# Head pairs in a second attention, and expert values accumulated with features in the partitions

## The reference

```python
s_w = jnp.einsum('bnqhgd,bnkhd->bnhgqk', qb, k_w).astype(jnp.float32) * scale
s_c = jnp.einsum('bnqhgd,bkhd->bnhgqk', qb, k_c).astype(jnp.float32) * scale
s_w = jnp.where(valid[None, :, None, None], s_w, NEG_INF)
p = jax.nn.softmax(jnp.concatenate([s_w, s_c, sink_b], axis=-1), axis=-1)
o = jnp.einsum('bnhgqk,bnkhd->bnqhgd', p_w, v_w) + jnp.einsum('bnhgqk,bkhd->bnqhgd', p_c, v_c)
```

```python
h = jnp.einsum('thkd,td->thk', u_tab[expert], zb).astype(jnp.float32)
act = (gate * jax.nn.gelu(h, approximate=False)).astype(zb.dtype)
return jnp.einsum('thk,thkd->td', act, v_tab[expert])
```

## Time and profile before

| | us |
|---|---|
| median of 3 runs | 4268.56 |
| lowest, highest | 4261.12, 4279.62 |
| the profiled execution | 4257.62 |
| its span, first to last instruction | 4255.8 |
| TensorE busy | 3832.7 (90%) |
| VectorE busy | 2633.9 (62%) |
| ScalarE busy | 1667.1 (39%) |
| GpSimd busy | 624.1 (15%) |
| mean granted clock of TensorE | 0.978 |

### The profile page before, as it was taken

How to read it: one execution, slowest core, us unless ns; L and a number is a source line. 1 busy time by engine, 2 the same in 40 slices (tenths; PEclk the granted TensorE clock), 3 DMA queues, 4 the chain that set the end, 5 groups by cost and what they waited for, 6 DMA issues and landing times. The chain is left out here.

```text
span 4255.8 us, 50533 instructions
## 1 busy us (share of the span) xinstructions
PE 3832.7 (90%) x17626; PEld 2701.9 (63%) x17626; DVE 2633.9 (62%) x5211; ACT 1667.1 (39%) x3644; POOL 624.1 (15%) x665
## 2 busy tenths in 40 slices
PE   6999988999999999998999888788789998887877
PEld 4788765788788865897878744233278787442322
DVE  6877556677565546656347666777553466677774
ACT  3222535323332245543225444444332254444443
POOL 1100000000000000000000143444300002444442
PEclk9999998999999999999999999999999999999999
DMA  5554111355333310553033599999920346999997
GB/s 213 202 184 173 70 40 55 119 181 171 128 141 131 125 61 1 199 186 120 11 129 129 220 420 420 420 420 420 375 80 21 129 146 248 420 420 420 420 420 310
DMA packets 135007, 904.29 MB, mean 212 GB/s; under 512 B 14855, under 2 KB 15879, under 8 KB 35168
## 3 DMA queue, kind: packets, MB, share of 16 engines
q0 software_dynamic: 95552, 620.97, 36.2%
q1 hardware_dynamic: 39200, 280.08, 18.5%
HBM read 899.90 MB, written 5.28 MB: 213 GB/s over the span
## 5 line engine op out<-in xcount | busy, mean ns | idle before, releaser
L2511 PE MATMUL ps<-arena 128*128 128x512 f32 x1640 | 809.8, 622 | 183.1 <-ACT arena L2574 181.5
L2670 DVE CUSTOM_DVE_ANT_0 arena<-arena 128x1024 f32<-128x1024 f32 x410 | 502.5, 1226 | 326.6 <-DMA arena<-peer_uv,arena 325.5
L620 DVE TENSOR_TENSOR w_lo<-wt,w_hi 128x1024 fp32r<-128x1024 f32 x388 | 475.4, 1225 | 351.7 <-ACT w_hi L602 328.1
L2511 PEld LDWEIGHTS ps<-arena 128*128 128x128 f32 x1640 | 292.4, 193 | 628.4 <-ACT arena L2574 402.0
L655 PE MATMUL ps<-h_hi,w_hi 128*128 128x512 f32 (+1 forms) x1744 | 649.4, 372 | 32.5 <-DVE h_lo L742 22.5
L2642 POOL DMA_INDIRECT arena<-peer_uv,arena x410 | 433.4, 1057 | 1583.3 <-DVEq L2633 989.2
L602 ACT ACTIVATE w_hi<-wt 128x1024 fp32r<-128x1024 f32 x388 | 407.6, 1058 | 636.1 <-PE ps L655 607.0
L655 PE MATMUL ps<-h_lo,w_hi 128*128 128x512 f32 (+1 forms) x1744 | 639.5, 367 | 0.0
L655 PE MATMUL ps<-h_hi,w_lo 128*128 128x512 f32 (+1 forms) x1744 | 639.2, 367 | 0.0
L450 PE MATMUL ps<-hT,wt 128*128 128x256 f32 x1632 | 407.0, 387 | 6.1 <-ACT hT L1389 5.1
L655 PEld LDWEIGHTS ps<-h_hi,w_hi 128*128 128x128 f32 x1744 | 332.1, 190 | 94.0 <-issue 17.7
(11 more groups left out here) (342 smaller groups left out, 5453.8 us busy)
## 6 DMA issues: line engine op xcount, KB each, us to landing
wt<-wstream SPq DMA_DIRECT2D x262, 1024.0 KB, 4.9
ada_t<-adastream POOLq DMA_DIRECT2D x133, 512.0 KB, 3.7
arena<-peer_uv,arena POOLq DMA_INDIRECT x410, 20.3
arena<-adastream POOLq DMA_DIRECT2D x11, 512.0 KB, 26.6
bias_by_query<-bias_by_distance POOLq DMA_DIRECT2D x1, 4096.0 KB, 17.3
arena<-bias_by_query POOLq DMA_DIRECT2D x1, 3072.0 KB, 12.1
xT<-tokens SPq DMA_DIRECT2D x1, 2048.0 KB, 15.2
cst<-consts SPq DMA_DIRECT2D x1, 1816.0 KB, 9.0
```

The lines of the kernel that those rows point to most:

```text
L620: self.step(self.dve.tensor_tensor(lo, raw_group(g), hi.bitcast(F32), ALU.subtract))
L2511: ins = pe.matmul(bank, diag[n % DIAGS], row[:, at:at + 512], start=s == 0, stop=s == SLOTS - 1)
L2670: dve.tensor_tensor_reduce(u, u, ztok[:, t], 1.0, 0.0, ALU.mult, ALU.add, hbuf[:, t, s:s + 1]).then_inc(dot_ready.sem, 1)
```

## The change

It makes two edits. In the second joint attention a unit becomes a pair of heads (16 pairs): both heads' scores go to two neighbouring banks, two pairs of banks rotate, the maximum is taken of both at once, the two turn banks serve one pair and are copied out in one instruction, and the values of the two heads go to the two halves of the partitions of one bank. The sink is negated once, and its exponent is formed on VectorE. In the expert layer the roles of the two operands are swapped: the row's 128x128 pieces are the weights and `diag` moves, eight matmuls of 128 columns in place of two of 512, so that the result has features in the partitions, and VectorE adds the banks to `xT` directly. The copy, the transposes and their two signals are gone.

```diff
         oB = MB(8, LAT)
-        N = Carve(U.at)
+        N = Carve()
         b_gain = small[:, 8:9]
-        b_banks = [ps[:, i] for i in range(4)]
-        b_probs = [N(TOK) for _ in range(3)]
-        sinkv = N(8, 4)
-        B_UNITS = [(h, q) for h in range(B_HEADS) for q in range(QT)]
+        b_probs = [N(2, TOK) for _ in range(3)]
+        b_mixed = [N(2, TOK) for _ in range(3)]
+        b_turned = [N(2, 4, P) for _ in range(3)]
+        sinkv = N(8, 4, 2)
+        sink_neg = N(B_HEADS)
+        assert N.at <= SPLIT_END
+        B_PAIRS = [(u, q) for u in range(B_HEADS // 2) for q in range(QT)]
...
         def pe_b_attend(pe, W, mm):
-            n = len(B_UNITS)
+            n = len(B_PAIRS)
             for i in range(n + LAG + 1):
                 if i < n:
-                    h, q = B_UNITS[i]
-                    r = slice((h % 2) * HD, (h % 2 + 1) * HD)
-                    bank, far = b_banks[i % 4], slice((1 - q) * P, (2 - q) * P)
-                    if i >= 4:
-                        pe.wait_ge(SB.raised, i - 3)
-                    mm(bank, qB[r, h // 2, q * P:(q + 1) * P], kD[r, h // 4, :], True, False)
-                    mm(bank[:, far], ident, const("window", q, TOK)[:, far], False, True, SB.scored)
+                    u, q = B_PAIRS[i]
+                    s, far = a_banks[i % 2], slice((1 - q) * P, (2 - q) * P)
+                    if i >= 2:
+                        pe.wait_ge(SB.raised, i - 1)
+                    for x in range(2):
+                        r = slice(x * HD, (x + 1) * HD)
+                        mm(s[:, x, :], qB[r, u, q * P:(q + 1) * P], kD[r, u // 2, :], True, False)
+                    for x in range(2):
+                        mm(s[:, x, far], ident, const("window", q, TOK)[:, far], False, True, SB.scored if x else None)
                 if LAG <= i < n + LAG:
                     u = i - LAG
-                    a, t = a_mixed[u % 3], turn_banks[u % 2]
                     pe.wait_ge(SB.even, u + 1)
-                    for j in range(4):
-                        ins = pe.transpose(t[:, j * P:(j + 1) * P], a[:, j * P:(j + 1) * P], ident)
+                    if u:
+                        pe.wait_ge(SB.kept, u)
+                    for x in range(2):
+                        for j in range(4):
+                            ins = pe.transpose(turn_banks[x][:, j * P:(j + 1) * P],
+                                               b_mixed[u % 3][:, x, j * P:(j + 1) * P], ident)
                     ins.then_inc(SB.turned, 1)
                 if i > LAG:
                     u = i - LAG - 1
-                    h, q = B_UNITS[u]
-                    g = h // 4
-                    r = slice((h % 2) * HD, (h % 2 + 1) * HD)
-                    t, o = turned[u % 4], value_banks[u % 2]
+                    g = B_PAIRS[u][0] // 2
+                    t, o = b_turned[u % 3], value_banks[u % 2]
                     pe.wait_ge(SB.kept, u + 1)
                     if u >= 2:
                         pe.wait_ge(SB.stored, u - 1)
                     for j in range(4):
-                        mm(o[r, 0:P], vB[:, j, g * HD:(g + 1) * HD], t[:, j, :], j == 0, j == 3,
-                           SB.valued if j == 3 else None)
+                        for x in range(2):
+                            mm(o[x * HD:(x + 1) * HD, 0:P], vB[:, j, g * HD:(g + 1) * HD], t[:, x, j, :], j == 0, j == 3,
+                               SB.valued if j == 3 and x else None)
...
         def act_b_attend(act):
-            n = len(B_UNITS)
+            n = len(B_PAIRS)
             for i in range(n + LAG):
                 if i >= LAG:
                     u = i - LAG
                     act.wait_ge(SB.turned, u + 1)
-                    act.activation(turned[u % 4], turn_banks[u % 2].rearrange("p (a b) -> p a b", b=P),
+                    act.activation(b_turned[u % 3], ps[:, 4:6].rearrange("p x (a b) -> p x a b", b=P),
                                    ACT.Copy).then_inc(SB.kept, 1)
                 if i < n:
-                    h, q = B_UNITS[i]
-                    sv = sinkv[:, i % 8, :]
+                    sv = sinkv[:, i % 8]
                     act.wait_ge(SB.peaked, i + 1)
-                    act.activation(b_probs[i % 3], b_banks[i % 4], ACT.Exp, bias=sv[:, 0:1], accum_out=sv[:, 1:2])
-                    act.activation(sv[:, 2:3], v("b_sink", h), ACT.Exp, bias=sv[:, 0:1]).then_inc(SB.raised, 1)
+                    for x in range(2):
+                        act.activation(b_probs[i % 3][:, x, :], a_banks[i % 2][:, x, :], ACT.Exp, bias=sv[:, 0, x:x + 1],
+                                       accum_out=sv[:, 1, x:x + 1])
+                    act.activation(sv[:, 2, :], sv[:, 2, :], ACT.Exp).then_inc(SB.raised, 1)
 
         def dve_b_attend(dve, step):
-            n = len(B_UNITS)
+            step(dve.tensor_scalar(sink_neg, v("b_sink", 0, B_HEADS), -1.0, None, ALU.mult))
+            n = len(B_PAIRS)
             for i in range(n + LAG + 2):
                 if i < n:
-                    h, q = B_UNITS[i]
-                    sv = sinkv[:, i % 8, :]
+                    u, q = B_PAIRS[i]
+                    sv, sink = sinkv[:, i % 8], sink_neg[:, 2 * u:2 * u + 2]
                     dve.wait_ge(SB.scored, i + 1)
-                    top = step.mark(dve.tensor_reduce(sv[:, 0:1], b_banks[i % 4], AX, ALU.max))
+                    top = step.mark(dve.tensor_reduce(sv[:, 0, :], a_banks[i % 2], AX, ALU.max, negate=True))
                 if i >= LAG + 2:
                     x = i - LAG - 2
-                    hx, qx = B_UNITS[x]
-                    r = slice((hx % 2) * HD, (hx % 2 + 1) * HD)
+                    ux, qx = B_PAIRS[x]
                     dve.wait_ge(SB.valued, x + 1)
-                    dve.tensor_copy(oB[r, hx // 2, qx * P:(qx + 1) * P], value_banks[x % 2][r, 0:P]).then_inc(SB.stored, 1)
+                    dve.tensor_copy(oB[:, ux, qx * P:(qx + 1) * P], value_banks[x % 2][:, 0:P]).then_inc(SB.stored, 1)
                 if i < n:
                     step.reached(top)
-                    dve.tensor_scalar(sv[:, 0:1], sv[:, 0:1], v("b_sink", h), -1.0, ALU.max, ALU.mult).then_inc(SB.peaked, 1)
+                    step.reached(step.mark(dve.tensor_tensor(sv[:, 0, :], sv[:, 0, :], sink, ALU.min)))
+                    dve.tensor_tensor(sv[:, 2, :], sv[:, 0, :], sink, ALU.subtract).then_inc(SB.peaked, 1)
                 if 1 <= i < n + 1:
-                    u = i - 1
-                    su = sinkv[:, u % 8, :]
-                    dve.wait_ge(SB.raised, u + 1)
-                    step.reached(step.mark(dve.tensor_tensor(su[:, 3:4], su[:, 1:2], su[:, 2:3], ALU.add)))
-                    step.reached(step.mark(dve.reciprocal(su[:, 3:4], su[:, 3:4])))
-                    dve.tensor_scalar(a_mixed[u % 3], b_probs[u % 3], su[:, 3:4], None, ALU.mult).then_inc(SB.even, 1)
+                    w = i - 1
+                    su = sinkv[:, w % 8]
+                    dve.wait_ge(SB.raised, w + 1)
+                    step.reached(step.mark(dve.tensor_tensor(su[:, 3, :], su[:, 1, :], su[:, 2, :], ALU.add)))
+                    step.reached(step.mark(dve.reciprocal(su[:, 3, :], su[:, 3, :])))
+                    for x in range(2):
+                        ins = dve.tensor_scalar(b_mixed[w % 3][:, x, :], b_probs[w % 3][:, x, :], su[:, 3, x:x + 1], None,
+                                                ALU.mult)
+                    ins.then_inc(SB.even, 1)
...
-        def pe_peer_out(pe, t):
-            pe.wait_ge(y_stored.sem, y_stored.due(pe, 2))
-            for half, bank in enumerate(out_banks(t)):
-                for k in range(4):
-                    m = 4 * half + k
-                    ins = pe.transpose(bank[:, k * P:(k + 1) * P], ztok[:, t, m * P:(m + 1) * P], ident)
-                ins.then_inc(y_turned.sem, 1)
...
-                if (t, h) == (1, 1):
-                    pe_peer_out(pe, 0)
...
                     pe.wait_ge(diag_ready.sem, diag_ready.due(pe))
-                    for bank, at in zip(y_banks(t), (D, D + 512)):
-                        ins = pe.matmul(bank, diag[n % DIAGS], row[:, at:at + 512], start=s == 0, stop=s == SLOTS - 1)
+                    for m in range(DC):
+                        ins = pe.matmul(y_banks(t)[m // 4][:, (m % 4) * P:(m % 4 + 1) * P], row[:, D + m * P:D + (m + 1) * P],
+                                        diag[n % DIAGS], start=s == 0 and m % 4 == 0, stop=s == SLOTS - 1,
+                                        skip_group_check=True)
                     ins.then_inc(row_free, 1)
                     n += 1
                 if scoring:
                     pe_peer_subs(pe, W, mm, l, h + AHEAD, 1)
-            pe_peer_out(pe, 1)
             pe_peer_sums(pe, mm, 1)
...
-                if h == PEER_H - 1:
-                    act.wait_ge(row_free, n)
-                    for half, bank in enumerate(y_banks(t)):
-                        act.activation(ztok[:, t, half * 512:(half + 1) * 512], bank,
```

(14 more changed lines are left out.)

## The result

The changed kernel takes 4237.53 us (median of 5 runs, 4227.70 to 4238.62) against 4268.56 beside it (4261.12 to 4279.62): a ratio of 0.9921, interval 0.9901 to 0.9941, so 25 to 42 us less (by the two medians 31.0). Forecast were 4232 and 4216 to 4252. The profiled execution took 4227.7 us, 29.9 less than that of before; 36.6 were forecast.

What follows compares the result with a forecast made beforehand. TensorE alone bounds the second attention, DMA the expert gathers. Attention 32.9 us off plus stage ends 3.7 makes 36.6, taking the profiled execution from 4257.6 to 4221.0 and the median from 4268.6 to 4232; range 4216 to 4252.

Steps and rivals of the forecast that it cites:

- Period: Second attention: a pair takes TensorE 3.56 us (scores 1.06, windows 0.43, transposes 1.05, values 1.02), where two units took 5.85.
- Fill: Start of the second attention: with only two score banks, pair 2 starts at 5.1 us and pair 5 at 13.9.
- Other engines: Second attention: VectorE about 3.1 us a pair at most and ScalarE about 2.7, both below TensorE's 3.56.
- The slots: Expert gathers: slots stay below DMA's 2.49 us, 2.21 with a query; nothing charged, bounds 0 to 31 us.
- The ends: End of both layers' gather stages: VectorE adds right after the last matmul, 1.83 us off each, 3.7 together.
- The clock at the end: Sums behind layer 1's gathers, earlier at mean clock 0.59: whether it falls there now is unknown, 1.6 us either way.
- rival 1: Expert gathers: TensorE becomes the bound, a pass takes 0.21 us instead of 0.11; 555 us more, 4787; chance 0.07.
- rival 2: Second attention: the two heads' values don't run side by side; period 4.42 us, stretch 74.3, time 4245; chance 0.12.
- Rival 3: Expert gathers: TensorE falls behind in query slots by more than buffers hold; 8 to 40 us given back; chance 0.11.

Runs made afterwards that it cites:

- experiment 3: Changed kernel with each head's window matmul directly after its own score, so a pair's scores are no longer neighbours; 4264.27 us, ratio 0.9992, attention stretch 89.22 us.
- experiment 4: Changed kernel with a pair's value matmuls ordered first head, then second head, instead of alternating; 4243.64 us, ratio 0.9928 to the kernel before, attention stretch 69.60 us.
- experiment 5: Changed kernel with window mask and identity copied to float32r, so each window matmul is one pass instead of two; 4234.17 us, ratio 0.9926, attention stretch 60.53 us.
- experiment 7: Changed kernel with one, or three, extra unread 128x128 matmuls per expert slot; 4235.00 us (ratio 0.9911) with one, 4309.98 us (ratio 1.0078) with three.

## Why the prediction was right

It was right in the total and in what carries it, the attention by pairs; the interval of 25 to 42 us holds the 36.6 forecast. The terms, in the order of the sum:

- **Period, 3.56 forecast, 3.60 measured.** Scores 1.06 and values 1.02 as summed, windows 0.44 for 0.43, transposes 1.07 for 1.05. The prices were rows of the same form elsewhere in this kernel, and experiments 3 and 4 show that the two large ones rest on the order of the instructions, experiment 5 that a pass less is a pass gained.
- **Fill, 13.9 us forecast to pair 5, 15.0 measured.** The chain was as drawn; pairs 2 and 5 of after's weight loads:
```profile
1605.19 0.30 PEld L450 LDWEIGHTS ps<-arena 64*128 64x128 f32 x4 [1.91 <-ACT arena L1324]
1606.89 0.93 PEld L450 LDWEIGHTS ps<-cst 128*128 128x128 f32 x4 [1.40 <-issue]
...
1614.99 0.30 PEld L450 LDWEIGHTS ps<-arena 64*128 64x128 f32 x4 [0.17 <-issue]
```
Pair 2 comes at 5.19 after the start (forecast 5.1). Then scores take 1.70 where others take 1.06 and four window loads 0.93 where others take 0.52: the clock stood at the lower level just there, and the pairs behind it were late. The two traces of experiment 7 have the same attention with the same waits and no such fall; the same loads and the whole stretch in the first of them:
```profile
1608.12 0.30 PEld L450 LDWEIGHTS ps<-arena 64*128 64x128 f32 x4 [1.91 <-ACT arena L1324]
1609.18 0.52 PEld L450 LDWEIGHTS ps<-cst 128*128 128x128 f32 x4 [0.76 <-issue]
...
1616.77 0.30 PEld L450 LDWEIGHTS ps<-arena 64*128 64x128 f32 x4 [0.17 <-issue]
```
```profile
1602.93:1664.83 61.90, 58.43 (x512) 40.11 (x512) 45.23 (x129) 39.57 (x96) 0.00 (x0) 1.00 0.01 2
```
There the scores of pair 2 take 1.06, pair 5 comes at 13.84 after the start, and the stretch is 61.9 at clock 1.00. So the fill was sized rightly, the 1.1 us are the clock, and a wait of TensorE in the fill does not bring the fall about each time. At equal clock the gain is 32.4 where 32.9 was forecast; the rest is the period. In after's trace the stretch is 63.05 and the gain 31.3, but the fall ahead of the attention was shorter there: the part of the stage ahead of it took 22.95 us at a mean clock of 0.85, against 24.31 at 0.79 before. Both together are 32.6 us shorter.
- **Other engines.** VectorE and ScalarE were forecast near 80% in the steady part. Eight rounds of it:
```profile
1620.40:1649.18 28.78, 28.78 (x258) 20.01 (x257) 22.14 (x64) 19.62 (x48) 0.00 (x0) 1.00 0.01 1
```
That is 77% and 68%, or 2.77 us a pair for VectorE, where I had 3.1 with waits on its own results, and 2.45 for ScalarE, where I had 2.7. Neither sets the period.
- **The slots, 0 charged.** A query slot of 2.21 was forecast and 2.22 measured. A pass takes 0.11, about a quarter of the 0.43 of 512 columns, with rows as weights that DMA has just written; a load adds next to nothing. The Trainium skill's rule in TensorE: Matmul & The Clock Gate, Part 3: Packing small matmuls, that loads overlap only where the row group differs, is not borne out for these full-height float32 loads either.
- **The ends, 2 x 1.83 forecast.** Measured 1.75 (3.85 to 2.10) in layer 0 and 1.77 in layer 1. The last slot's 16 passes of 128 columns run 0.06 longer than four of 512, which I had left out. The gather stages are 2.4 and 3.8 us shorter as a whole, 1.5 of the latter from the clock in the norm's sums (next point).
- **The clock at the end, 1.6 us either way.** It went the good way: 16 loads 1.86 us instead of the 3.36 of the earlier trace rows. In 4214 to 4218 the clock is 1.00. That is luck as far as the forecast goes. With the old expert part these loads took 3.36, 3.41 and 1.86 in three traces; with the new one 1.86 in all eight, and whether the change keeps the clock up there was not tested.

The rivals: rival 1 (0.21 per pass) is refuted by the 0.11, and rival 2 by 16 loads in 0.85; experiment 4 shows what a worse order looks like, 0.49 us a pair where the rival had 0.86. Rival 3 is refuted by 1.01 and 419 in the full windows and by gather stages that became shorter, and experiment 7 says how near it was, 0.27 us per query slot. By the two profiled executions the stages that the change touches are 37.4 us shorter (31.3, 2.4 and 3.8), where 36.6 were forecast; 1.5 of the 37.4 are the clock of the last point. At equal clock the attention and the two ends come to 32.4 and 3.5, 35.9 in all. 7.5 us came back in stages that no edit touches, which leaves 29.9. That last part changes sign when the other two executions are paired: 4275.8 against 4232.2 is 43.6 us. One price on record does not come out of its own working: for rival 3, a quarter to all of 0.06 x 512 = 31 us and as much again are, taken literally, 15 to 61 us and not 8 to 40; the forecast's sum does not use it.

## What to carry to other kernels

Take the price of a new instruction pattern from a row of the same shape and the same order elsewhere in the trace, and place matmuls that can share the array directly behind each other: one loop line was worth some 20 of 32 us at equal clock. Where DMA bounds a stage, work added to another engine is free up to a margin that can be measured by adding dummy work until the rate falls; state that margin per slot in the stage's worst part, not as a mean. Before explaining a few microseconds, in stages that no edit touches or in one that an edit does, compare the granted clock of the stretch in both traces, and profile the old kernel a second time.

## What the runs showed that was not expected

- TensorE runs passes of another output half ahead by some four passes: 16 passes in head order take 1.34 us, where the alternating order takes 0.85.
- A change of the array's shape costs 0.17 to 0.19 us at clock 1.00 where it was read, around the values and in experiment 3; at clock 0.50 the same idle time before the value loads is 0.33.
- The changed kernel has 62,653 instructions and fetches 3.08 MB of them, 0.8 MB more than before, beside full DMA engines; no stage shows a cost of it.
- The same 656 passes of one kernel took 98.2 and 104.5 us in two executions, at clocks 0.94 and 0.86. The same attention took 63.05 and 61.9 us, at 0.97 and 1.00.
- Under a TensorE bound the DMA share stays at 0.94 to 0.98 while the rate falls from 419 to between 348 and 372 GB/s: the rate is the number to read.
